# Token halves at the four boundaries behind the output and down projections of a three-block transformer kernel

## The reference, cut to what matters

```python
mixed = concat([tok, mem_out]) @ w_out[i]          # output projection
x = x + rms_norm(mixed, norm_mix_post[i])
h = rms_norm(x, norm_ffn_pre[i])
gu = h @ w_gu[i]                                   # gate and up
f = (silu(gu[..., :D_FF]) * gu[..., D_FF:]) @ w_down[i]   # down projection
x = x + rms_norm(f, norm_ffn_post[i])
```

## Time and profile before

| | before |
|---|---|
| median of 3 runs | 1948.34 us (1947.86 to 1948.65) |
| profiled execution, its own time | 1947.74 us |
| its span | 1945.9 us |
| TensorE (PE) busy | 1927.0 us, 99% |
| VectorE (DVE) busy | 971.4 us, 50% |
| ScalarE (ACT) busy | 774.5 us, 40% |
| GpSimd (POOL) busy | 182.4 us, 9% |

### The profile page before, as it was taken

How to read it: one execution, slowest core, us unless ns; L and a number is a source line. 1 busy time by engine, 2 the same in 40 slices (tenths; PEclk the granted TensorE clock), 3 DMA queues, 4 the chain that set the end, 5 groups by cost and what they waited for, 6 DMA issues and landing times.

```text
span 1945.9 us, 24129 instructions
## 1 busy us (share of the span) xinstructions
PE 1927.0 (99%) x9956; PEld 1568.2 (81%) x9956; DVE 971.4 (50%) x1464; ACT 774.5 (40%) x1252; POOL 182.4 (9%) x197
## 2 busy tenths in 40 slices
PE   9999999999999999999999999999999999999997
PEld 7967788888878867788888887878888888888886
DVE  5575665553227366565554227343665556425522
ACT  5386433333423176433333325233764443212321
POOL 4111300000105030210000003000000020000000
PEclk9999999999999999999999999999999999999999
DMA  6421223333333221233333333331212333322322
GB/s 192 142 60 44 86 90 97 96 97 100 92 101 99 94 64 34 80 99 93 97 97 98 94 101 108 98 109 44 77 30 87 111 98 98 98 95 94 96 96 85
DMA packets 52117, 178.72 MB, mean 92 GB/s; under 512 B 6380, under 2 KB 7788, under 8 KB 51880
## 3 DMA queue, kind: packets, MB, share of 16 engines
q1 hardware_dynamic: 49656, 169.14, 27.7%
q0 software_dynamic: 2208, 7.97, 1.5%
q10 hardware_dynamic: 144, 0.06, 0.0%
HBM read 174.48 MB, written 2.66 MB: 91 GB/s over the span
## 4 chain that ended last, share of the span: by engine, by line
PE 96%; DVE 2%; ACT 1%; issue 0%; DMA 0%; SPq 0%; DVEq 0%; ACTq 0%
PE bank L1516 24%; PE bank L1517 23%; PE bank L1518 23%; PE bank L1760 3%; PE bank L1717 2%; PE bank L1682 2%; PE bank L1535 2%; PE bank L1536 2%; PE bank L1537 2%; PE bank L1430 1%; PE bank L1422 1%; PE bank L1425 1%; PE bank L1574 1%; PE bank L1575 1%; PE bank L1576 1%; PE bank L1594 1%
## 5 line engine op out<-in xcount | busy, mean ns | idle before, releaser
L982 DVE TENSOR_TENSOR w_lo<-w_raw,w_hi 128x1024 fp32r<-128x1024 f32 (+2 forms) x325 | 403.9, 1244 | 733.9 <-ACT w_hi L566 733.4
L566 ACT CAST w_hi<-w_raw 128x1024 fp32r<-128x1024 f32 (+2 forms) x325 | 328.5, 1012 | 581.3 <-DMA w_raw<-in_w_down 133.7
L1516 PE MATMUL bank<-h_hi,w_hi 128*128 128x512 f32 x1288 | 503.0, 391 | 0.2 <-DVE q_buf L1048 0.2
L1517 PE MATMUL bank<-h_lo,w_hi 128*128 128x512 f32 x1288 | 501.8, 390 | 0.0
L1518 PE MATMUL bank<-h_hi,w_lo 128*128 128x512 f32 x1288 | 501.8, 390 | 0.0
L1516 PE MATMUL bank<-a_hi,w_hi 128*128 128x512 f32 (+1 forms) x752 | 289.4, 385 | 0.0
L1517 PE MATMUL bank<-a_lo,w_hi 128*128 128x512 f32 (+1 forms) x752 | 289.2, 385 | 0.0
L1518 PE MATMUL bank<-a_hi,w_lo 128*128 128x512 f32 (+1 forms) x752 | 289.1, 384 | 0.0
L1516 PEld LDWEIGHTS bank<-h_hi,w_hi 128*128 128x128 f32 x1288 | 242.0, 188 | 53.4 <-DVE w_lo L982 1.6
L1518 PEld LDWEIGHTS bank<-h_hi,w_lo 128*128 128x128 f32 x1288 | 242.2, 188 | 50.8
L1517 PEld LDWEIGHTS bank<-h_lo,w_hi 128*128 128x128 f32 x1288 | 242.2, 188 | 49.8
(11 more groups left out here) (232 smaller groups left out, 2313.4 us busy)
## 6 DMA issues: line engine op xcount, KB each, us to landing
w_raw<-in_w_gu SPq DMA_DIRECT2D x88, 512.0 KB, 3.5
w_raw<-in_w_mlp_in SPq DMA_DIRECT2D x32, 512.0 KB, 3.5
w_raw<-in_w_mlp_out SPq DMA_DIRECT2D x32, 512.0 KB, 3.5
w_raw<-in_w_down SPq DMA_DIRECT2D x32, 448.0 KB, 3.3
w_raw<-in_w_out SPq DMA_DIRECT2D x24, 512.0 KB, 3.6
w_raw<-in_w_down SPq DMA_DIRECT2D x16, 512.0 KB, 3.6
w_raw<-in_w_gates SPq DMA_DIRECT2D x16, 512.0 KB, 3.5
w_raw<-in_w_qk_b SPq DMA_DIRECT2D x14, 512.0 KB, 3.6
```

What stands on the lines that cost most here:

```text
L566: nc.scalar.copy(slot(w_hi, v), slot(w_raw, v)).then_inc(w_hi_done, 1)
L982: nc.vector.tensor_tensor(slot(w_lo, v), slot(w_raw, v), slot(w_hi, v).bitcast(F32), ALU.subtract).then_inc(w_split, 1)
L1516: mm(acc, w1, hi, start=start, stop=False)
L1517: mm(acc, w1, lo, start=False, stop=False)
```

## The change

The last tile of `w_out` and `down` is computed for tokens 0 to 255 ("left") first, in bank 3, and then for tokens 256 to 511 ("right"), in bank 0; for `down` this holds within each of the three weight units. The statistic is made for the left half as soon as it is there, in the middle of the right half's matmuls, and again for the right half in the middle of the next stage's first matmuls. VectorE adds the last square to the sum of seven, so TensorE makes one sum of 256 columns for each half in place of two of 512. The scale, add, lead, trail and stair matmuls of chunks 0 to 3 are done for the left half, then for the right half; chunks 4 to 7 as before in one piece. ScalarE copies six tiles out of PSUM in place of four. `keep_busy` goes.

```diff
             def read_f(n, b, f, at_, gain, turned_layer=None):
                 def read(k, acc, done):
+                    if k == DC - 1:
+                        act.wait_ge(half_done, b + 1)
+                        act.wait_ge(sq_pooled, stat_count(n) + DC - 2)
+                        nc.scalar.activation(sq[:, 1, halves[0]], acc[:, halves[0]], ACT.Square).then_inc(half_sq, 1)
+                        return
                     act.wait_ge(unit_done, done)
                     square_streamed(n, k, acc[:, :])
-                    if k < 4:
+                    if k < 6:
...
+            def leads(n, b, gain, split, last_tile, last_acc, acc):
+                left, right = halves
+                for c in range(4):
+                    act.wait_ge(half_x, 4 * b + c + 1)
+                    lead(c, xT[:, c, left], h_hi[:, c, left], gain, half_hi)
+                    if c == 0:
+                        act.wait_ge(unit_done, last_tile)
+                        nc.scalar.activation(sq[:, 1, right], last_acc[:, right], ACT.Square).then_inc(sq_done, 1)
+                    elif c == 2:
+                        act.wait_ge(sq_summed, n)
...
                 for c in range(DC):
                     act.wait_ge(x_ready, n_x[0] - DC + c + 1)
-                    lead(c, xT[:, c, :], h_hi[:, c, :], gain)
+                    if c < 4:
+                        lead(c, xT[:, c, right], h_hi[:, c, right], gain)
+                    else:
+                        lead(c, xT[:, c, :], h_hi[:, c, :], gain)
...
+                dve.wait_ge(half_sq, b + 1)
+                dve.wait_ge(sq_pooled, stat_count(n + 1))
+                square_sum(left)
...
+                dve.wait_ge(half_rstd, b + 1)
+                update(0)
+                update(1)
+                for i in range(12):
+                    if i < 4:
+                        trail(i, xT[:, i, left], h_hi[:, i, left], h_lo[:, i, left], pre, (half_hi, half_ready, 4 * b))
+                        if i == 0:
+                            dve.wait_ge(sq_done, DC * (n + 1))
+                            square_sum(right)
+                    elif i < 8:
+                        trail(i - 4, xT[:, i - 4, right], h_hi[:, i - 4, right], h_lo[:, i - 4, right], pre)
+                    else:
+                        trail(i - 4, xT[:, i - 4, :], h_hi[:, i - 4, :], h_lo[:, i - 4, :], pre)
+                    update(i + 2)
...
-            def keep_busy(times, u):
...
+            def last_tile(st, rhs, first_sum):
+                banks = bank_of(st, side[0], DC - 1), bank_of(st, side[0], 0)
+                pe.wait_ge(acc_read_act, n_act[0] + 5)
+                pieces = st.tiles[DC - 1]
+                for i, (u, first, m) in enumerate(pieces):
+                    pe.wait_ge(w_split, u + 1)
+                    for half in range(2):
+                        cols, acc = halves[half], banks[half][:, halves[half]]
+                        for c in range(m):
...
+                            if end and half == 0:
+                                last.then_inc(half_done, 1)
+                            if half and c == m - 1:
+                                last.then_inc(unit_done, 1)
+                            if half and i == len(pieces) - 1 and c == 2:
+                                first_sum()
...
-                    add_seven(n, ps[old + 3])()
-                    add_last(n, ps[old + 3])
-                    keep_busy(14, after)
+                    def first_sum():
+                        wait_reads(freed[-1])
...
+                        sum_half(0, ps[old + 3], 2 * b + 1, half_summed)
```

More of the change, by code:

```diff
@@ L1007, in add_normed @@
-            def add_normed(n, f, at_, f_side, post, pre, turned_layer=None):
-                def scaled(c):
-                    if c < 4:
[L1011 to L1025, removed]
+                                               ALU.mult, ALU.subtract).then_inc(ready, 1)
@@ L1040, in add_normed, with update @@
-                n_td[0] += DC
+                        x_old = x_moved[:, c, cols]
+                    nc.vector.tensor_tensor(xT[:, c, cols], x_old, scaled(c, cols), ALU.add).then_inc(made, 1)
+                def update(i):
+                    if i < 4:
+                        scale(i, left)
+                        add(i, left, half_x)
+                    elif i < 8:
+                        if i == 4:
+                            dve.wait_ge(rstd_done, n + 1)
+                        scale(i - 4, right)
+                        add(i - 4, right, x_ready)
+                    elif i < 12:
+                        scale(i - 4, whole)
+                        add(i - 4, whole, x_ready)
@@ new lines, in square_sum @@
+                def square_sum(cols):
+                    nc.vector.tensor_tensor(sq[:, 1, cols], sq_sum[:, cols], sq[:, 1, cols], ALU.add).then_inc(half_added, 1)
+                dve.wait_ge(half_sq, b + 1)
+                dve.wait_ge(sq_pooled, stat_count(n + 1))
+                square_sum(left)
+                if turned_layer is not None:
+                    lo_to(down[turned_layer].after(DC - 1) + 2)
+                dve.wait_ge(half_rstd, b + 1)
+                update(0)
+                update(1)
@@ L1407, in chunk_order @@
                 if not st.stair:
-                    plain = [(k, i, c) for k, tile in enumerate(st.tiles) for i, (_, _, m) in enumerate(tile)
+                    tiles = st.tiles[:DC - 1] if st in w_out + down else st.tiles
+                    plain = [(k, i, c) for k, tile in enumerate(tiles) for i, (_, _, m) in enumerate(tile)
                              for c in range(m)]
@@ L1495, in dense, with sum_half @@
+            def sum_half(half, acc, count, made):
+                cols = halves[half]
+                pe.wait_ge(half_added, count)
+                mm(acc[:, cols], ones[:, :], sq[:, 1, cols], start=True, stop=True).then_inc(made, 1)
+            def dense(st, rhs, reads, wait_rhs=lambda chunk: None, hooks={}, begun=(), boundary=None):
                 begin_side()
                 seen = 0
-                if st.stair:
+                if boundary:
+                    stairs_by_halves(st, rhs, *boundary)
+                elif st.stair:
```

163 lines of the change are left out of this document (126 added, 37 removed).

## The result

The changed kernel takes **1957.56 us** (median of 5 runs, 1957.05 to 1958.04) against 1948.34 us before (5 runs, 1947.63 to 1948.95): ratio 1.0048, 95% interval 1.0033 to 1.0062. It is slower by 9.2 us; 1955 was forecast, with a range from 1948 to 1961. The profiled execution took 1958.03 us, its span is 1956.2 us (before 1947.74 and 1945.9), its mean granted clock 0.995 (before 0.998).

The account below looks back on a forecast made before the run. VectorE, working without pause from its first scale to tile 3's `w_lo`, was taken to bound the boundaries. Tile 3 at +1.0 us behind `w_out` and +2.4 behind `down`, twice each, gave +6.8 us: 1955, range 1948 to 1961.

Parts of the forecast that it names:

- What bounds the kernel: At the boundaries: VectorE works without pause from first scale to tile 3's `w_lo`; TensorE's slack against it is small.
- When the first scale starts: Left square behind the cast, its sum behind `w_lo`: first scale 0.86 us earlier behind `w_out`, 0.48 later behind `down`.
- How long VectorE works: First scale to tile 3's `w_lo`: +1.9 us (half chunks +1.68, right square sum +0.345, chunks 4 and 5 -0.12).
- TensorE's clock: Rival: without `keep_busy` the clock falls in TensorE's new gaps, 1 to 3 us each boundary, 1959 to 1967; chance 0.10.
- The sum: Tile 3 +1.0 us behind each `w_out`, +2.4 behind each `down`: +6.8 us over four boundaries, forecast 1955.
- The cast does not stand in the way: Rival: first scale at about 211.6, TensorE's stairs and splits the bound, -4 us in all, 1944; chance 0.12.
- Cheaper halves: Rival: VectorE's halves cost less or the trail beside GpSimd shrinks; boundary kinds cancel, 1948 to 1951; chance 0.18.

Follow-up runs that it names:

- the one with the late cast: Changed kernel with cast and `w_lo` behind the left square, only two chunks halved, right square and sum ahead of the stairs, one VectorE addition dropped: 1945.61 us.
- the one with the sum last: Version with two halved chunks and cast and `w_lo` ahead of the left square, with the left half's sum put behind the right half's last matmul: 1953.78 us.
- the cast moved: Changed kernel with ScalarE's cast of the last weight unit and VectorE's `w_lo` put behind the left half's square and its sum: 1947.78 us.
- two halved chunks and the early cast: Version with two halved chunks, but cast and `w_lo` ahead of the left square as in the changed kernel: 1958.59 us.

## Why the prediction was right, point by point

*What bounds the kernel.* Right, and shown by two runs: VectorE bounds the boundaries (halving its work alone costs 4.4 us), and the cast and `w_lo` in the queues decide when it starts (moving them gives back 9.8 us). The two do not share the loss, though. Measured from the start of the last tile the first scale moved by -0.59, +0.66, -0.71 and +0.64 us, 0.0 in all: the queues cost the change its gain, and what it lost against the kernel before is VectorE's 4 x 1.9 = 7.6 us and the clock.

*When the first scale starts.* Right in mechanism and place, a little early. The new wait is 2.47 us (forecast 2.5), ended by VectorE's addition. Measured from the start of the last tile, the scale comes 0.59 us earlier than before; forecast was 0.86. The 0.27 are the cast, which starts 0.09 later, and the handovers from engine to engine: addition to sum 0.57 in place of 0.48, sum to Ln 0.70 in place of 0.63. I had taken 0.03 to 0.06 us for a handover that took up to 0.15 (from the addition's end, 212.59, to the sum, 212.74). At the other three boundaries the term was 0.18, 0.15 and 0.16 off, about 0.8 us in all.

*How long VectorE works.* +1.9 us was forecast; at three boundaries the first scale to tile 3 went from 19.80 to 21.7. The terms came from rows of instructions of just that width, and they held within 0.12 us: 8 x 1.19 - 4 x 1.99 = 1.56 for the half chunks (1.68 taken), 0.34 for the right square sum, 0.12 less for chunks 4 and 5. That makes 1.8. The last 0.13 are the split scale of chunk 7, a term that I did not have. That the sum is exact is luck.

*TensorE's clock.* This step failed. From the end of the program I argued that 4 us of idle are borne, and gave a fall a chance of 0.10. It fell at one boundary of four (1.3 us) and once more at 1290 us. I had also read the row of 9s as a full clock. A 9 stands for 90% or more, and a slice is 49 us long. Stretches of the kernel before, with the granted clock:

```profile
1213.00:1214.00 1.00, 1.00 (x5) 0.77 (x4) 1.00 (x2) 0.11 (x2) 0.00 (x0) 0.93 0.00 0
1214.00:1215.00 1.00, 1.00 (x4) 0.77 (x3) 1.00 (x2) 0.00 (x0) 0.00 (x0) 0.50 0.00 0
```

So the clock fell inside that kernel too, where TensorE was busy by its records; it had just done 16 matmuls of one column (1209.94 to 1212.5). That row would have warned me. `keep_busy` was not free: without it the kernel before loses 4 us. By the Trainium skill (TensorE: Matmul & The Clock Gate, The HAM clock gate), which I had set against the change and weighed too low, an idle engine falls back to the lower clock; these runs agree, with 3.84 us idle and 0.50 from within it on.

*The sum.* 6.8 forecast, 10.3 us of span measured; the 3.5 between are 0.8 for the first scales, 1.3 for the clock at the second boundary, and 1.4 for the rest of the program, with the fall at 1290 in it. That last part is not the change's, as far as the traces show. From tile 3 of the fourth boundary to the end all eleven traces have one or two falls, the first at 1209 to 1226, the second at 1277 to 1290. The three with both (the change, and of the runs with two halved chunks the one with the late cast and the one with the sum last) take 757.3 us there, the eight with one 755.5 to 755.9, kernels with `keep_busy` and without among them. Why one execution has the second fall and another not, no run settles. So the mechanism held for 7.6 us and the clock added some 2.7, of which 1.3 lie at the boundaries.

*Rivals.* "The cast does not stand in the way" is refuted by the row of the cast, 3.00 us idle ended by a DMA. My price for it was wrong as well: with the cast moved I had 211.6 for the first scale and 1944 us, and the run gave 212.50 and 1947.8, since Ln and the scale queue behind the same two instructions and VectorE still has its 1.9 us. "Cheaper halves" is refuted by 1.19 us a half chunk (1.205 taken): 0.12 us a boundary, where that rival needed 1.0 us or more.

## What to carry to other kernels

Splitting a statistic so that half of it can start early gains nothing while the instruction that feeds it stands in an in-order queue behind one that waits for a transfer; look at what stands ahead of it in the queue of every engine it passes, and move that first. Splitting also bills the engine that has no slack for the fixed part of each instruction, so split only as many chunks as cover the second half's latency: here two, together with the earlier second sum and one addition less, did better than four, and one did worse. A waiting instruction moved out of one queue place lands in another, so ask what the engine does in the last microseconds before the critical stretch, its clock included.

## What the runs showed of the hardware that I had not expected

**The clock did not follow the length of the idle alone.** The same wait for the half sum was borne in one run and not in another: in the changed kernel 2.35, 2.47 and 2.78 us were borne and 2.80 was not; with two halved chunks and the early cast 2.37, 2.43 and 2.79 us were followed by a half clock and 2.80 was not. Idles of 2.67 us right ahead of the stairs (with 0.54 to 1.41 us shortly before) fell four times of four, 3.84 us four times of four; with the moved cast 1.70 us was borne and 1.82 us was not. Shorter ones did not save it either: with the sum last, the first boundary has three idles of 0.63, 0.85 and 0.49 us and fell, the third has 0.49, 0.85 and 0.49 and did not. The plainest case is one that no edit touches: an idle of 1.80 us in `softmax`, the same in all eleven traces, was followed by a half clock in six and not in five. Each trace is of one execution. So a wait of 2 to 3 us in TensorE has to be priced as a fall that may come or not, and a shorter one is not safe. Added over slices of one microsecond, one fall took 1.7 or 3.4 us off the clock, but a boundary only grew by what came on top of VectorE's bound, from nothing to 2.0 us in these traces.

**Cutting an instruction of 512 columns on VectorE into two adds 0.09 us on average when the halves stand together** (0.07 for scale and addition, 0.76 against 0.69 us busy, and 0.13 for the trail, 0.87 against 0.74), **and 0.13 when each waits for the one before.**
